# Two stacked transformer blocks on one core: leading units without the norm's scale, two norms as one, layer 1 without meta columns

## What is computed

```python
def rmsnorm(x, g):
    y = xf * lax.rsqrt(jnp.mean(xf * xf, axis=-1, keepdims=True) + EPS)
    return (y * g.astype(jnp.float32)).astype(x.dtype)

def first_block(...):
    h = jnp.concatenate([meta, x], axis=1)
    for l in range(DEPTH):
        h = h + 0.5 * swiglu(rmsnorm(h, norm_gains[l, 0]), ...)
        h = h + mixer(rmsnorm(h, norm_gains[l, 1]), ...)
        h = h + 0.5 * swiglu(rmsnorm(h, norm_gains[l, 2]), ...)
    return rmsnorm(h, final_norm)[:, N_META:]

def second_block(...):
    for l in range(DEPTH):
        h = rms_norm(x, ln1_g[l]) * (1.0 + sc1) + sh1
        z = h @ w_in[l]
...
        x = x + g1 * (merged @ w_out[l])
        h2 = rms_norm(x, ln2_g[l]) * (1.0 + sc2) + sh2
        x = x + g2 * (jnp.square(jax.nn.relu(h2 @ w_ff1[l])) @ w_ff2[l])
    return rms_norm(x, final_g)
```

## Time and profile before

| | |
|---|---|
| three runs | 2155.3, 2156.64, 2156.89 us (median 2156.64) |
| the profiled execution's own time | 2157.01 us |
| its span | 2155.7 us |
| PE busy | 2071.2 us (96%), 15,686 matmuls |
| PE weight loads, beside them | 1959.0 us (91%) |
| DVE / ACT busy | 1401.6 (65%) / 980.0 us (45%) |
| chain that ended last | PE 91%, DVE 4%, ACT 3% |
| mean granted clock of PE | 0.971 of full speed |
| DMA | 363.24 MB, 169 GB/s in the mean |

### The profile page before, as it was taken

The page is one execution under the profiler, slowest core; times in us unless marked ns, Lnnn a source line. Parts: engine busy times, 40 slices in busy tenths (PEclk is TensorE's granted clock), DMA queues, the critical chain, the costliest instruction groups (busy, mean ns, idle before and its releaser), DMA issues.

```text
span 2155.7 us, 37123 instructions
## 1 busy us (share of the span) xinstructions
PE 2071.2 (96%) x15686; PEld 1959.0 (91%) x15686; DVE 1401.6 (65%) x2296; ACT 980.0 (45%) x1555; POOL 38.8 (2%) x56
## 2 busy tenths in 40 slices
PE   7999999999999999999999999989999998999998
PEld 6999888799999999978789999978899998889998
DVE  5776454368775777555437777566688556668854
ACT  5443344354443444345344544255644335564432
POOL 0000000000000000000000000030000003000000
PEclk9999998899999999999999999999999999999999
DMA  6774322145775577522214676333445553354553
GB/s 234 266 281 173 116 81 79 59 137 198 271 267 187 196 254 263 186 84 93 79 64 171 235 254 257 128 120 103 157 157 194 178 169 120 104 174 159 189 183 118
DMA packets 50830, 363.24 MB, mean 169 GB/s; under 512 B 6534, under 2 KB 7974, under 8 KB 8680
## 3 DMA queue, kind: packets, MB, share of 16 engines
q1 hardware_dynamic: 50664, 360.86, 47.5%
HBM read 359.78 MB, written 1.05 MB: 167 GB/s over the span
## 4 chain that ended last, share of the span: by engine, by line
PE 91%; DVE 4%; ACT 3%; issue 1%; DMA 0%; SPq 0%; DVEq 0%
PE bank L391 25%; PE bank L393 25%; PE bank L392 24%; PE bank L575 2%; PE bank L648 1%; PE bank L421 1%; PE bank L661 1%; PE bank L425 1%; PE bank L422 1%; ACT w_hi L979 1%; PE bank L620 1%; PE bank L527 1%; PE bank L466 1%; DVE full L1394 1%; PE bank L557 1%
## 5 line engine op out<-in xcount | busy, mean ns | idle before, releaser
L391 PE MATMUL bank<-xn_hi,w_hi 128*128 128x272 f32 (+1 forms) x2832 | 830.3, 293 | 1.6 <-DVE w_lo L1352 1.6
L393 PE MATMUL bank<-xn_lo,w_hi 128*128 128x272 f32 (+1 forms) x2832 | 817.5, 289 | 0.0
L392 PE MATMUL bank<-xn_hi,w_lo 128*128 128x272 f32 (+1 forms) x2832 | 815.3, 288 | 0.0
L391 PEld LDWEIGHTS bank<-xn_hi,w_hi 128*128 128x128 f32 x2832 | 539.3, 190 | 23.1 <-issue 21.3
L392 PEld LDWEIGHTS bank<-xn_hi,w_lo 128*128 128x128 f32 x2832 | 539.4, 190 | 1.0
L393 PEld LDWEIGHTS bank<-xn_lo,w_hi 128*128 128x128 f32 x2832 | 539.1, 190 | 0.1
L1352 DVE TENSOR_TENSOR w_lo<-raw_a,w_hi 128x1024 fp32r<-128x1024 f32 (+1 forms) x280 | 352.3, 1261 | 162.1 <-ACT w_hi L979 160.7
L1352 DVE TENSOR_TENSOR w_lo<-raw_b,w_hi 128x1024 fp32r<-128x1024 f32 (+2 forms) x282 | 357.7, 1272 | 145.6 <-ACT w_hi L979 144.3
L979 ACT ACTIVATE w_hi<-raw_b 128x1024 fp32r<-128x1024 f32 (+2 forms) x282 | 307.8, 1093 | 273.9 <-PE bank L393 233.6
L979 ACT ACTIVATE w_hi<-raw_a 128x1024 fp32r<-128x1024 f32 (+1 forms) x280 | 302.7, 1084 | 273.1 <-PE bank L393 225.8
L393 PE MATMUL bank<-h_lo,w_hi 128*128 128x272 f32 x704 | 203.1, 289 | 0.0
(11 more groups left out here) (292 smaller groups left out, 2698.3 us busy)
## 6 DMA issues: line engine op xcount, KB each, us to landing
raw_b<-in_weights SPq DMA_DIRECT2D x123, 1024.0 KB, 4.8
raw_a<-in_weights SPq DMA_DIRECT2D x121, 1024.0 KB, 4.8
ada_raw<-in_ada_w SPq DMA_DIRECT2D x48, 1024.0 KB, 4.9
raw_a<-in_weights SPq DMA_DIRECT2D x16, 1408.0 KB, 5.8
raw_b<-in_weights SPq DMA_DIRECT2D x16, 1408.0 KB, 5.7
raw_b<-in_weights SPq DMA_DIRECT2D x2, 1152.0 KB, 5.2
raw_a<-in_weights SPq DMA_DIRECT2D x2, 640.0 KB, 4.3
cst<-in_const SPq DMA_DIRECT2D x1, 1152.0 KB, 8.7
```

The lines of the kernel that those rows point to most:

```text
L391: pe.matmul(o, wh, xh, start=start, stop=False)
L392: pe.matmul(o, wl, xh, start=False, stop=False)
L393: return pe.matmul(o, wh, xl, start=False, stop=stop)
```

## The change

**Leading units.** For the first two units of each stage, `xn_hi` and `xn_lo` are now made of `x * gain`, without `rstd`, tile by tile as the previous stage writes `x` (`before_norm`). `norm_sum` stands behind the fourth k-tile of these units. Their output tiles are multiplied by `rstd` on DVE when they are read (`gate` in the FFNs, `qa`, `cq`, and `full` in `ff`). In the second block the shift cannot be added to an unscaled `x`; it goes in as two more columns (258 in place of 256), and the column of products that it gives is added after the scale (`shift_column`, `shifted`). Units u+2 and u+3 run interleaved behind them with the normalised `x`, as u and u+1 did before. The held splits now stand ahead of the norm.

**Two norms as one.** For ln1_0 a second sum is kept, of the squares of `x` times `fn`'s gain. One `norm_sum` has both, `two_norms` makes both roots and their product, and `in_place` of `fn` moves behind the first output tiles.

**Meta columns.** In layer 1 the 16 meta columns are left out of what no token column needs afterwards: the mixer's units 8 to 11 and 14 to 49, all of `ffn(1,1)`, the meta queries of the attention and the meta tile of the GLA.

**Moved beside it.** At the start `v1` is loaded first and `x` in four pieces, the sums of squares run inside the leading units, and the rotary angles move to a later place. `log_gates` runs behind unit 3 of a mixer in place of unit 1. `y` has buffers of its own. The second block's vectors are loaded once.

```diff
+LIVE = [TA] * (L - 1) + [TB]
+LIVE_TILES = [TILES] * (L - 1) + [TILES[1:]]
...
+            if lead is not None:
+                if kk < KD - 1:
+                    m.then_inc(*k.up("lead_mm", (stage, kk)))
+                lead(kk)
+
+    def leading_units(u, cols, to, stage):
+        def norm(kk):
...
+            elif kk == 3:
+                norm_sum(7, cols, stage)
+        tiles_as_ready(u, 0, to if to == cols else slice(0, N + 2), c.xn_hi, c.xn_lo, ("g", *stage), norm)
+        tiles_as_ready(u + 2, 2, to, c.xn_hi, c.xn_lo, stage)
...
-                for t, (c0, n) in enumerate(TILES):
+                for c0, n in LIVE_TILES[l]:
                     m = pe.matmul(bank[b][0:n, c0:c0 + n], c.kinv[hr, i, c0:c0 + n], c.qdec[hr, i, c0:c0 + n], start=True, stop=True)
...
-                for t, (c0, n) in enumerate(TILES):
-                    m = pe.matmul(o[:, 0:META], c.vb[0:n, t, g * 64:g * 64 + 64], c.lt[0:n, t, lc:lc + META], start=t == 0, stop=t == 2)
+                if live == TA:
+                    for t, (c0, n) in enumerate(TILES):
+                        m = pe.matmul(o[:, 0:META], c.vb[0:n, t, g * 64:g * 64 + 64], c.lt[0:n, t, lc:lc + META], start=t == 0, stop=t == 2)
...
     def mixer(l):
-        norm_sum(7, TA, stage)
-        chains = [(1, 4, log_gates(l)), (6, 34, gla(l)), (8, 38, attention(l))]
+        leading_units(u0, TA, TA, stage)
+        chains = [(3, 6, log_gates(l)), (6, 34, gla(l)), (8, 38, attention(l))]
...
-                tile(u0 + u, b, T, c.xn_hi, c.xn_lo)
+                tile(u0 + u, b, TA if u == 12 else live, c.xn_hi, c.xn_lo)
...
# ScalarE
+    def before_norm(stage, kk, gain, cols, to):
+        act.activation(c.xn_hi[:, kk, to], c.x[:, kk, cols], ACT.Copy, scale=gain[:, kk:kk + 1]).then_inc(*k.up("x_hi", ("g", *stage, kk)))
+
+    def normalised(stage, to, held, bias=None):
+        split_hi(held)
+        split_hi(held + 1)
...
+            if kk < KD - 1:
+                act.wait_ge(*k.at("lead_mm", (("g", *stage), kk)))
+            else:
+                act.wait_ge(k.sem["unit_done"], held)
...
-            if kk in (3, 5):
-                split_hi(held + kk // 5)
...
# VectorE
+        split_lo(held)
+        split_lo(held + 1)
+        if stage == ("ln1", 0):
+            two_norms(stage)
         dve.wait_ge(*k.at("rstd", stage))
...
-        split_lo(held)
-        split_lo(held + 1)
         dve.memset(c.sumsq[:, :], 0.0).then_inc(*k.up("sums"))
...
+    def before_norm(stage, kk, gain, cols, to):
+        hi = c.xn_hi[:, kk, to]
+        dve.wait_ge(*k.at("x_hi", ("g", *stage, kk)))
+        dve.scalar_tensor_tensor(out=c.xn_lo[:, kk, to], in0=c.x[:, kk, cols], scalar=gain[:, kk:kk + 1], in1=hi.bitcast(F32),
+                                 op0=ALU.mult, op1=ALU.subtract).then_inc(*k.up("x_lo", ("g", *stage, kk)))
...
     def ffn(l, f, after):
...
+        for j in range(2):
+            dve.wait_ge(k.sem["unit_done"], u + j + 1)
+            dve.tensor_tensor(c.gate[:, j, cols], bank[j][:, cols], c.rstd[:, cols], ALU.mult).then_inc(*k.up("tile_v", ("gate", l, f, j)))
...
     def mixer2(l):
-        normalised(stage, TB, c.gain[:, 0, :], u0 + 2, bias=c.mod[:, 0:8])
+        normalised(stage, TB, TN, c.gain[:, l, 0, :], u0 + 2, bias=c.mod_all[:, l, 0:8])
+        for j in range(2):
+            cq = c.cq[:, j, :]
+            dve.tensor_tensor(cq, bank[j][:, TN], c.rstd[:, TB], ALU.mult).then_inc(*k.up("tile_v"))
+            shifted(j, j)
+            dve.tensor_scalar(cq, cq, c.shift[:, j:j + 1], None, ALU.add).then_inc(*k.up("tile_v", ("cq0", l, j)))
+        if l == 0:
+            in_place(TB, c.vg[:, G_FN:G_FN + 8], c.rstd2[:, :], "fn")
+            gains(1)
```

More of the change, by code:

```diff
@@ L579, in gla @@
             take(2)
-            pe.matmul(bank[2][:, 0:T], c.ones, c.sq[:, :], start=True, stop=True).then_inc(*k.up("gla_mm", ("sum", l, h)))
+            pe.matmul(bank[2][:, LIVE[l]], c.ones, c.sq[:, LIVE[l]], start=True, stop=True).then_inc(*k.up("gla_mm", ("sum", l, h)))
             free[2] = [("gla_a", ("root", l, h))]
@@ L698, in mixer @@
             if u < 4:
[L699 to L703 removed]
+                free[u] = [("tile_v" if u < 2 else "tile_a", ("qk", l, u))]
             elif u < 8:
@@ new lines, in shift_column, with from_input, square @@
+    def shift_column(l, first):
+        act.wait_ge(*k.at("mod_v", ("gain", l)))
+        for i in range(2):
+            act.activation(c.xn_hi[:, :, N + i], c.mod_all[:, l, first:first + 8], ACT.Copy).then_inc(*k.up("x_hi", ("shift", l, first, i)))
+    def from_input():
+        gain = c.v1[:, V_GAIN:V_GAIN + 8]
+        def square(kk):
+            if kk > 1:
+                act.wait_ge(*k.at("square_mm", kk - 2))
+            act.activation((c.sq, c.sq2)[kk % 2][:, :], c.x[:, kk, :], ACT.Square).then_inc(*k.up("square_a", kk))
+        act.wait_ge(*k.at("vec_in", (1, 0)))
+        for kk in range(KD):
+            if kk % 2 == 0:
+                act.wait_ge(*k.at(f"x_in_{kk // 2}", 0))
+            before_norm(("ffn", 0, 0), kk, gain, TA, TA)
+            if kk == 1:
+                split_hi(0)
+                split_hi(1)
+            if kk > 1:
+                square(kk - 2)
+        square(KD - 2)
+        square(KD - 1)
+        act.wait_ge(*k.at("ones_in", 0))
@@ new lines, in shift_column, with shifted, gains @@
+    def shift_column(l, first):
+        for i in range(2):
+            low(c.xn_lo[:, :, N + i], c.mod_all[:, l, first:first + 8], c.xn_hi[:, :, N + i], ("shift", l, first, i))
+    def shifted(j, b):
+        dve.tensor_copy(c.shift[:, j:j + 1], bank[b][:, N:N + 1]).then_inc(*k.up("tile_v"))
+    def gains(l):
+        for i, (g, sc) in enumerate(((V_LN1, 8), (V_LN2, 32))):
+            o = c.gain[:, l, i, :]
+            dve.scalar_tensor_tensor(out=o, in0=c.mod_all[:, l, sc:sc + 8], scalar=1.0, in1=c.v2[:, l, g:g + 8], op0=ALU.add,
+                                     op1=ALU.mult).then_inc(*k.up("mod_v", ("gain", l) if l and i else None))
+        if l == 0:
+            dve.wait_ge(*k.newest("mod_v"))
+            o = c.gain[:, 0, 0, :]
+            dve.tensor_tensor(o, o, c.vg[:, G_FN:G_FN + 8], ALU.mult).then_inc(*k.up("mod_v", ("gain", 0)))
```

590 lines of the change are left out of this document (335 added, 255 removed).

## The result

The changed kernel takes **2096.88 us** in the median of 4 runs (2092.75 to 2102.54), the kernel before 2156.67: ratio 0.9726, interval 0.9702 to 0.975. Forecast were 2121, with 2098 to 2140: the direction is right, the gain is 59.8 us where 35.5 were said, and the time lies just outside the range. A second job gave 2102.88 for the same kernel, so its runs spread over more than 10 us. They go in the order of their mean granted clock: 2092.75 us at 0.984, 2095.37 at 0.983, 2098.38 at 0.981, 2102.54 at 0.979. Why that clock differs is part of the story.

A forecast was written before the change was run, and what follows sets the result against it. PE, busy 96% of the span, was taken as the bound. From 2157.0 us, 8.7 for stage changes net of clock loss and 26.8 for meta columns were taken, giving 2121.5, forecast as 2121, range 2098 to 2140.

The forecast's parts named there:

- Stage changes: At nine stage changes and the start, leading units let PE go on: 19.1 us gained, 8.7 net of clock loss.
- ffn10's terms: At the ffn10 stage change, the chain with the table load was said to end at 17.9 us, gaining 0.6.
- what stands ahead of the norms: In PE's wait table, nearly all its idle time was said to stand ahead of the norms.
- Meta columns: In layer 1's mixer and ffn(1,1): 16.8 us from shorter products and 10.0 from dropped small matmuls, together 26.8.
- The rival in which weight loads set the pace: In layer 1, dropped columns give from nothing to half of 16.8 us: 2129 to 2138 us, chance 0.12.
- the estimate from the Trainium skill: For layer 1's products, 16 columns are worth 2.1 ns, 5.3 us in all, putting the time about 2132.
- Against it, the clock: Behind PE's new waits at stage changes, half-clock stretches cost 10.4 us in all, with bounds of nothing and 17.
- One price for a matmul: From windows in two undisturbed FFNs: 125.6 ns a matmul at 272 columns, 119.0 ns at 256, at full clock.
- the first rival: Stage changes pay more, as ACT finishes sooner or the clock does not fall: 2111, or 2090 to 2101; chance 0.22.

The follow-up runs named there:

- the kernel with all columns: The changed kernel with all 272 columns kept in layer 1, leaving the leading units, joint norm and start: 2137.1 us, ratio 0.9924.
- the early split: The changed kernel with the fifth unit's weight split moved earlier on ACT and DVE, ahead of the table load and the clearing of sumsq: 2090.99 us, ratio 0.9684.
- each variant: The changed kernel with only the attention's meta queries, or only the GLA's meta columns, kept in layer 1: 2109.77 and 2109.09 us; second time 2097.93 and 2108.55.
- The better version's second profile: The changed kernel with the early split except in mixers, one start activation table, later in-place norm and reordered latent sums: 2082.91 us, profiled run 2072.56.

## Why the prediction was wrong

- **Stage changes: right.** 19.1 us were summed for ten stages ahead of the clock. The windows give 18.5 for nine; the start lost 0.6 where 0.4 was to be won, as its waits came to 16.9 us in place of 15.5 (the first unit's `w_lo`, above). The half-clock stretches behind the new waits were charged with 10.4. Up to the end of the sixth unit the ten stages keep 8.4 us of the 17.9 (9.5 in the kernel with all columns), where 8.7 were forecast. The mechanism, fifth unit's weights behind eight `xn_hi` and the table load, is what the timeline shows, and the early split removed it. Two slips of the working cost nothing here: ffn10's terms add up to 17.7, not 17.9, and what stands ahead of the norms is some two thirds of PE's listed waits, not nearly all.
- **Meta columns: right, and a little low.** 26.8 were forecast. Mixer 1 gave 17.5 us with its clock taken off, and `ffn(1,1)` 11.1 behind its sixth unit, 28.6 together; 2.1 of it because the matmuls of `ffn(1,1)` took 117.7 ns, and not 119.0. The rival in which weight loads set the pace is out. With it the estimate from the Trainium skill, "TensorE: Matmul & The Clock Gate", section "Back-to-back issue gap" (5.3 us for the products), is out too: the 11.1 us of `ffn(1,1)` alone are more.
- **"Against it, the clock": the step that failed.** It priced half-clock stretches only where the change makes PE wait, as a loss, and put those that the mixers already had at nothing. The mixers had more of them than the stage changes: 34 and 17 us at half clock in the windows of 237.72 and 230.20 us (0.93 and 0.96), 41 us in the nine windows of the earlier trace rows. Mixer 1 lost all of its stretches, worth 230.20 - 222.66 = 7.5 us, mixer 0 one of its own, 3.0, by the run. A part that makes the smallest matmuls go should have been asked what it does to the clock beside them; the profile of before had the rows.
- **One price for a matmul.** 119.0 ns was taken for all 256-column products, and the second block behind the sixth units of its stages was priced at nothing. It gave 7.2 us: 3.4 by ff's down products (90.3 us for 92.0 in each layer), of which the place of `f` is at least a part; about 1.5 by a half-clock stretch less in one mixer; 1.8 by the mixers' output products, whose pace changes by the execution (last section). The rest is open.
- **The range.** The forecast's own parts gave 8.4 and 28.6 us, 1.5 more than was said of them. What it put at nothing, the mixers' clock (7.5 + 3.0 = 10.5) and the second block's 7.2, makes up the rest of the 54.5 us between the two profiled runs, to 0.2. So the time lies where the first rival was put (2090 to 2101), but not by its mechanism: PE did wait for the fifth unit's weights, and the clock fell behind six of the eight waits. The median lies 5.7 lower still, for the profiled run was the slowest: the forecast counted on runs that agree, as those of before did (2155.3 to 2156.89 in the runs shown). In later jobs before too spread, 2147.8 to 2162.39.

## What to carry to other kernels

Price the clock of every stage whose matmuls change, not only of those where the engine waits: read the granted clock stage by stage, and treat a stage below 1.00 as time that a change may give back or lose. Where an unscaled operand takes a norm off the path, the next in line is whatever still stands behind the norm on the other engines, here the next unit's weights: move them too. And where runs of one program differ by stretches of the clock, compare stages by profiles that share a clock before naming a cause; one profile of each variant named the wrong one here.

## What the runs showed of the hardware beside that

The same 1,598 matmuls of mixer 0 took 222.66 to 237.72 us, with no wait changed, by the granted clock alone. Matmuls of one shape differ by their operands' place: 64 bytes ahead of `f` moved 674 of them from 79.15 to 79.74 us. They differ without it too. The 192 output products of a second-block mixer took 22.55 us in both layers before; their right side then got a buffer of its own, and with the same buffers, both at full clock, they take 21.65 us in some executions and 22.49 in others. The better version's second profile has both, one in each layer:

```profile
1483.95:1505.60 21.65, 21.65 (x193) 21.65 (x192) 19.95 (x41) 10.90 (x17) 0.00 (x0) 1.00 0.49 170
1851.33:1873.82 22.49, 22.49 (x193) 22.49 (x192) 20.60 (x42) 10.88 (x17) 0.00 (x0) 1.00 0.46 161
```

What chooses between the two was not tried.
